# Token tile 2's transposed values copied out of PSUM by ScalarE, and the token differences moved behind the third ffn strip's weight split

## The chip, the cores and the metric

The kernel runs on one core of a Trainium2 chip. The metric is device time in microseconds (us) for one execution of the whole two-layer trunk. TensorE (PE in the profile, with its weight loads as PEld) does the matmuls, VectorE is DVE, ScalarE is ACT, GpSimd is POOL, and SyncE (SP) issues the DMAs. Each engine runs its own instruction list in order, and the lists are tied together by semaphores.

## What is computed

Two layers of a decoder trunk over 512 tokens of width 1024, in float32. The change lies between the first residual sum and the feed-forward part:

```
x = x + rms_norm(mix, norm_mix_post[i])
h = rms_norm(x, norm_ffn_pre[i])
gate, up = split_cols(h @ w_ffn_in[i], (D_FF, D_FF))     # D_FF = 2816: 22 strips of 128 columns
f = (jax.nn.silu(gate) * up) @ w_ffn_out[i]
x = x + rms_norm(f, norm_ffn_post[i])
```

## The kernel before

The tokens are handled in four tiles of 128 (m = 0 to 3). Every matmul operand is split into a rounded part and a remainder (`w_hi`, `w_lo` of the weights, `h_hi`, `h_lo` of the activations), and each product is three matmuls (lines 800 to 802). ScalarE writes the rounded part (line 1189 for weights, line 1225 for `h`), and VectorE subtracts it from the source to get the remainder (line 1603 for weights, line 1669 for `h`).

The order of the work is written out by hand: `plan_schedule` makes one list of events, and each engine walks through that same list and does its own share of each event. So an event's place in the list fixes what stands ahead of it on every engine that has a share in it.

For the ffn input, tile m goes through this chain. `post mix m` updates `x`. `pre ffn m` norms it: ScalarE takes a Square with its sum (line 1216), GpSimd turns the sum into a factor (lines 1481 and 1482), VectorE writes `xn` in two halves (line 1619). `T ffn m`: TensorE transposes `xn` into PSUM banks 2m and 2m+1 (line 993), ScalarE writes `h_hi`, VectorE writes `h_lo`.

The ffn strips 0, 1 and 2 (`f[0]`, `f[1]`, `f[2]`) are plain: a block `mm f[j] m` is 48 matmuls of 256 tokens, for token half m. Its first matmuls wait for the strip's `w_lo` (`lo_ready`, line 862). From strip 3 on, the kernel uses a scheme of seven products that needs, besides `h`, four combinations of `h` between the token halves, T_sum 1 to 4. The difference events make them on VectorE (`differences`, line 1673): `diff p 0` makes the first two from PSUM banks 4+2p and 5+2p (tile 2+p) and from `h_raw` (tile p), `diff p 1` makes the other two (lines 1680 and 1681). `h_raw` holds ScalarE's full-width copies of tiles 0 and 1 (event `hraw m`, line 1266); before each copy ScalarE waits until VectorE has read the same bank for `h_lo` (line 1265). Event `Tc` then splits T_sum into `T_hi` (line 1272) and `T_lo` (line 1767).

The block `mm f[2] 0` writes banks 4 and 5, where tile 2's transposed values lie, so it waits until `diff 0 0` has read them (line 955). SyncE loads the weights in pieces into five buffers, and reloads a buffer once VectorE has split the piece in it (line 775).

Of the kernel before, what the change touches and what calls it, by code (L numbers as in the profile page):

```python
# [16 lines left out]
F32 = mybir.dt.float32  # L17
# [7 lines left out]
P = 128  # L25
# [106 lines left out]
def plan_schedule(depth):  # L132


    ev = []
    strips = {kind: [s for s in STRIPS if s[0] == kind] for kind, _, _ in STRIPS}
    ins, o, f, fo, g = (strips[kind] for kind in ("in", "out", "ffn", "fo", "gate"))
    ple = ("ple", None, 0)
    layer = 0

    def add(*e, lay=None):
        ev.append((layer if lay is None else lay, e))

    def mm(strip, m, lay=None):
        add("mm", strip, m, lay=lay)

    def close(strip):

        add("conv", SIDX[strip] + SLOTS)

    def tail(pair, renew, after):

        lay = layer + (after == "mix")
        for m in range(TILES):
            mm(pair[0], m)
            if m >= 1:
                add(*renew, m - 1)
            if m >= 2 and after != "mix":  # L160
                add("T", after, m - 2, lay=lay)
                if m == TILES - 1 and after == "ffn":
                    add("hraw", 0)
                    close(pair[0])
            if m >= 1 and after == "ffn":
                add("pre", after, m - 1, lay=lay)
            if m == TILES - 1 and after != "ffn":
                close(pair[0])
            mm(pair[1], m)
            if m >= 1 and after == "mix" and lay < depth:  # L170
                add("T", after, m - 1, lay=lay)
                if m < TILES - 1:
                    add("pre", after, m - 1, lay=lay)

    for e in (("T", "mix", 0), ("conv", 0), ("mm", ins[0], 0), ("T", "mix", 1), ("pre", "mix", 0), ("T", "mix", 2),
              ("evac", ins[0], 0), ("pre", "mix", 1), ("mm", ins[0], 1), ("T", "mix", 3), ("conv", 1), ("pre", "mix", 2),
              ("evac", ins[0], 1), ("mm", ins[0], 2), ("pre", "mix", 3), ("mm", ins[0], 3), ("evac", ins[0], 2),
              ("conv", 2), ("mm", ins[1], 0), ("evac", ins[0], 3), ("mm", ins[1], 1)):
        add(*e)
    close(ins[0])  # L180
    for layer in range(depth):
        at = plan_mixers()
        u = 4
        for s in ins[1:]:
            for m in range(TILES):
                if u >= 6:
                    mm(s, m)
                for e in at.pop(u, ()):
                    add(*e)
                u += 1  # L190
            close(s)
        mm(o[0], 0)
        for u in (52, 53):
            if u == 53:
                mm(o[1], 0)
            for e in at.pop(u, ()):
                add(*e)
        add("gmlp_mix")
        mm(o[0], 1)
        mm(o[1], 1)  # L200
        add("gmlp_yT")
        mm(o[0], 2)
        mm(o[1], 2)
        assert not at, at
        mm(o[0], 3)
        close(o[0])
        mm(o[1], 3)
        close(o[1])
        tail(o[2:], ("post", "mix"), "ffn")
        add("post", "mix", 3)  # L210
        add("hraw", 1)
        add("hi", SIDX[f[2]])
        mm(f[0], 0)
        add("T", "ffn", 2)
        add("diff", 0, 0)
        add("pre", "ffn", 3)
        add("lo", SIDX[f[2]])
        add("diff", 0, 1)
        mm(f[1], 0)
        add("T", "ffn", 3)  # L220
        add("diff", 1, 0)
        add("diff", 1, 1)
        mm(f[2], 0)
        mm(f[0], 1)
        add("Tc")
        add("mid", 0)
        add("first")
        mm(f[1], 1)
        add("mid", 1)
        mm(f[2], 1)  # L230
        add("mid", 2)
        for j in FAST:
            add("step", j)
            if LAST - 5 <= j < LAST - 1:
                add("split", j - LAST + 5)
        add("last7")
        mm(fo[0], 3)
        add("last4")
        add("conv", SIDX[fo[1]])
        add("split", 4)  # L240
        add("split", 5)
        for m in (0, 1, 2):
            mm(fo[0], m)
        add("conv", SIDX[fo[2]])
        close(fo[0])
        add("split", 6)
        add("split", 7)
        for i in range(1, len(fo) - 2):
            for m in (2, 3, 0, 1):
                mm(fo[i], m)  # L250
            close(fo[i])
            for k in (2 * i + 6, 2 * i + 7):
                if k < FCH:
                    add("split", k)
        tail(fo[-2:], ("post", "ffn"), "gate")
        add("post", "ffn", 3)
        mm(ple, 0)
        add("T", "gate", 2)
        mm(ple, 1)
        add("T", "gate", 3)  # L260
        add("post", "ple", 0)
        mm(ple, 2)
        add("post", "ple", 1)
        close(fo[-1])
        mm(ple, 3)
        add("post", "ple", 2)
        add("post", "ple", 3)
        close(ple)
        for s in g[:2]:
            for m in range(TILES):  # L270
                mm(s, m)
            close(s)
        tail(g[2:], ("gated",), "mix")
        nxt = layer + 1
        if nxt < depth:
            add("gated", 3)
            mm(ins[0], 0, nxt)
            close(g[3])
            mm(ins[0], 1, nxt)
            add("T", "mix", 3, lay=nxt)  # L280
            add("pre", "mix", 2, lay=nxt)
            add("pre", "mix", 3, lay=nxt)
            mm(ins[0], 2, nxt)
            mm(ins[1], 0, nxt)
            mm(ins[1], 1, nxt)
            mm(ins[0], 3, nxt)
            add("conv", SIDX[ins[0]] + SLOTS, lay=nxt)
        else:
            add("gated", 3)
    return ev  # L290
# [44 lines left out]
def build_trunk(nc, depth, x_in, p_t, pre_mix, w_in, ln_w, ln_b, ws_t, bs_t, gn_w, sinks, w_out,  # L335
# [5 lines left out]
    def place(name, shape, dt, kb):  # L341
        return nc.alloc_sbuf_tensor_at(name, shape, dt, offset=BASE + int(kb * KB))
# [10 lines left out]
    T_sum = place("T_sum", [P, 4, 4, S // 2], F32, 64)  # L353
    ext_sum = place("ext_sum", [P, 3 * 512], F32, 130)
    h_raw = place("h_raw", [P, 2, 4, S // 2], F32, 116)
    ext_hi = place("ext_hi", [P, 3 * 512], F32R, 124)
    ext_lo = place("ext_lo", [P, 3 * 512], F32R, 130)
    w_sum = [place(f"w_sum{i}", [P, 2 * PIECE], F32, 172 + 8 * i) for i in range(SLOTS)]
# [372 lines left out]
    with nc.Block() as block:  # L731
# [66 lines left out]
        def _(pe):  # L798
# [133 lines left out]
            def block_of(layer, strip, m):  # L932
# [17 lines left out]
                    last = mm_rows(y_hi, y_lo, 2 * i, g, m, i == 3, i == 0)  # L950
                elif kind == "ffn":
                    if m == 0 and i < 2:
                        pe.wait_ge(h_raw_ready, 4 * layer + 2 * i + 2)
                    elif m == 0:
                        pe.wait_ge(t_raw, 8 * layer + 2)
                    last = mm_ffn(layer, g, strip, m)
                elif kind == "fo":
                    if i == 0 and m < 3:
                        pe.wait_ge((st_silu1, st_silu2, st_mid1)[m], nth(layer, LAST))
                    pe.wait_ge(mid_lo_ready, layer * FCH + 2 * i + 2)  # L960
                    last = mm_fo(g, i, m)
                elif kind == "ple":
                    pe.wait_ge(h_lo_ready, t_count(layer, "gate", m))
                    pe.wait_ge(p_lo_ready, layer + 1)
                    last = mm_rows(p_hi, p_lo, 0, g, m, True, True)
                else:
                    if i == 0:
                        pe.wait_ge(ple_ready, layer * TILES + m + 1)
                    if i == 3 and ends(layer, m):
                        last = mm_end(g)  # L970
                    else:
                        last = mm_rows(h_hi, h_lo, 2 * i, g, m, i == 0, i == 3)
# [185 lines left out]
        def _(act):  # L1158
# [90 lines left out]
            for layer, e in schedule:  # L1249
# [12 lines left out]
                elif kind == "hraw":  # L1262
                    m = e[1]
                    for half in range(2):
                        act.wait_ge(h_lo_ready, t_count(layer, "ffn", m, half))
                        act.activation(h_raw[:, half, :, m * P:(m + 1) * P],
                                       banks[2 * m + half][:, :].rearrange("p (k t) -> p k t", k=4),
                                       ACT.Copy).then_inc(h_raw_ready, 1)
                elif kind == "Tc":
                    for i in range(4):  # L1270
# [293 lines left out]
        def _(dve):  # L1564
# [108 lines left out]
            def differences(layer, p, part):  # L1673

                cols = slice(p * P, (p + 1) * P)
                top, low = (banks[4 + 2 * p + i][:, :].rearrange("p (k t) -> p k t", k=4) for i in range(2))
                t1, t2, t3, t4 = (T_sum[:, i, :, cols] for i in range(4))
                if part:
                    landed(combos["T2"])
                    done(dve.tensor_tensor(t3, t2, h_raw[:, 0, :, cols], ALU.subtract), t_raw)  # L1680
                    done(dve.tensor_tensor(t4, h_raw[:, 1, :, cols], t2, ALU.subtract), t_raw)
                    return
                dve.wait_ge(h_raw_ready, 4 * layer + 2 * p + 2)
                landed(done(dve.tensor_tensor(t1, top, h_raw[:, 0, :, cols], ALU.subtract), t_raw))
                combos["T2"] = done(dve.tensor_tensor(t2, low, t1, ALU.subtract), t_raw)

# [356 lines left out]
```

## Time and profile before

| | us |
|---|---|
| median of 3 runs | 1246.45 (1246.43 to 1246.53) |
| profiled execution, its own time | 1246.74 |
| its span in the profile | 1244.9 |
| TensorE busy in the span | 1236.6 |
| VectorE busy | 786.8 |
| ScalarE busy | 571.7 |
| GpSimd busy | 131.3 |

The profile is of one execution. The span is the time from its first to its last instruction; the profiled execution's own time has 1.84 us around it. A matmul's row shows a start and a modelled end that lies over the start of the next, so TensorE is best read by the starts of its matmuls. Times in rows are microseconds from the span's start. The stretch of interest lies at about 204 to 245 us in the first layer and at about 820 to 861 us in the second.

### The profile page before, as it was taken

The numbers are of one execution on the slowest core, as the hardware profiler recorded it, in microseconds if no ns is written. First come the engines' busy times: TensorE is split into PE (matmuls) and PEld (weight loads), VectorE is DVE, ScalarE is ACT, GpSimd is POOL, SyncE is SP. The second block draws the span as 40 slices with busy tenths as digits, with TensorE's granted clock in tenths as the row PEclk, the third lists the DMA queues.
The fourth block names the chain that finished last, engine by engine and source line by source line (L and its number), as shares of the span: only waits on it lengthen the run. The fifth ranks groups of instructions, "written<-read, shape, count | busy, mean of one in ns | idle before, by whom it ended". The sixth has DMA issues, their size and how long they took to land.

```text
span 1244.9 us, 20535 instructions
## 1 busy us (share of the span) xinstructions
PE 1236.6 (99%) x8045; PEld 1136.7 (91%) x8045; DVE 786.8 (63%) x1329; ACT 571.7 (46%) x1084; POOL 131.3 (11%) x225
## 2 busy tenths in 40 slices
PE   9999999999999999999999999999999999999998
PEld 7999888999999988888899989889999999888886
DVE  5575545888888843337466746368988887532463
ACT  6444334555555532235454444263655555322351
POOL 2003521100000000002120037120000000000020
PEclk9999999999999999999999999999999999999999
DMA  7322132233333353322232222231333332523211
GB/s 248 104 65 89 69 102 68 69 102 102 102 108 112 104 170 102 131 72 89 77 96 62 89 65 85 85 97 57 102 108 112 105 103 102 170 85 134 68 51 67
DMA packets 124206, 122.30 MB, mean 98 GB/s; under 512 B 5200, under 2 KB 109008, under 8 KB 124112
## 3 DMA queue, kind: packets, MB, share of 16 engines
q1 hardware_dynamic: 124112, 121.01, 31.2%
q8 instruction: 64, 1.05, 0.3%
q14 instruction: 30, 0.25, 0.1%
HBM read 118.90 MB, written 2.10 MB: 97 GB/s over the span
## 4 chain that ended last, share of the span: by engine, by line
PE 99%; DVE 0%; DMA 0%; SPq 0%; issue 0%; ACT 0%; ACTq 0%
PE bank L800 30%; PE bank L802 30%; PE bank L801 30%; PE bank L993 2%; PE bank L1050 1%; PE bank L1073 1%; PE bank L1119 1%; PE bank L1071 1%; PE bank L1103 1%; PE bank L1058 0%; PE bank L1095 0%; PE bank L1115 0%; DMA raw<-in_w_in 0%; PE bank L1124 0%; PE bank L1145 0%; PE bank L1032 0%
## 5 line engine op out<-in xcount | busy, mean ns | idle before, releaser
L800 PE MATMUL bank<-w_hi,h_hi 128*128 128x384 f32 (+2 forms) x672 | 244.0, 363 | 1.8 <-DVE w_lo L1605 1.8
L801 PE MATMUL bank<-w_lo,h_hi 128*128 128x384 f32 (+2 forms) x672 | 237.5, 353 | 0.0
L802 PE MATMUL bank<-w_hi,h_lo 128*128 128x384 f32 (+2 forms) x576 | 200.4, 348 | 0.0
L1603 DVE TENSOR_TENSOR w_lo<-raw,w_hi 128x1024 fp32r<-128x1024 f32 x86 | 102.4, 1230 | 150.0 <-ACT w_hi L1189 149.8
L1189 ACT ACTIVATE w_hi<-raw 128x1024 fp32r<-128x1024 f32 x86 | 86.7, 1055 | 174.5 <-PE bank L802 174.4
L800 PE MATMUL bank<-h_hi,w_hi 128*128 128x256 f32 x568 | 161.0, 284 | 0.5 <-issue 0.5
L802 PE MATMUL bank<-h_hi,w_lo 128*128 128x256 f32 x568 | 160.7, 283 | 0.0
L801 PE MATMUL bank<-h_lo,w_hi 128*128 128x256 f32 x568 | 160.7, 283 | 0.0
L800 PEld LDWEIGHTS bank<-w_hi,h_hi 128*128 128x128 f32 x672 | 126.4, 188 | 15.5 <-issue 1.7
L802 PE MATMUL bank<-w_hi,mid_lo 128*128 128x512 f32 x352 | 137.0, 389 | 0.0
L801 PEld LDWEIGHTS bank<-w_lo,h_hi 128*128 128x128 f32 x672 | 126.6, 188 | 10.7
L800 PE MATMUL bank<-T_hi,w_hi 128*128 128x256 f32 x448 | 126.8, 283 | 0.0
L801 PE MATMUL bank<-T_lo,w_hi 128*128 128x256 f32 x448 | 126.8, 283 | 0.0
L802 PE MATMUL bank<-T_hi,w_lo 128*128 128x256 f32 x448 | 126.8, 283 | 0.0
L802 PEld LDWEIGHTS bank<-w_hi,h_lo 128*128 128x128 f32 x576 | 108.3, 188 | 7.6
L800 PEld LDWEIGHTS bank<-h_hi,w_hi 128*128 128x128 f32 x568 | 109.0, 192 | 1.0 <-issue 0.9
L801 PEld LDWEIGHTS bank<-h_lo,w_hi 128*128 128x128 f32 x568 | 109.0, 192 | 0.1
L802 PEld LDWEIGHTS bank<-h_hi,w_lo 128*128 128x128 f32 x568 | 109.0, 192 | 0.0
L1247 ACT ACTIVATE w_hi<-w_sum 128x512 fp32r<-128x512 f32 x112 | 70.5, 629 | 52.5 <-DVE w_sum L1703 51.2
L1502 POOL TENSOR_SCALAR tiny<-tiny 128x1 f32<-128x1 f32 x24 | 13.1, 544 | 763.8 <-ACT junk_f L1340 676.0
L1605 DVE SCALAR_TENSOR_TENSOR w_lo<-raw,mix_col,w_hi 128x384 fp32r<-128x384 f32 (+2 forms) x112 | 63.6, 630 | 38.1 <-ACT w_hi L1189 38.1
L800 PEld LDWEIGHTS bank<-T_hi,w_hi 128*128 128x128 f32 x448 | 86.0, 192 | 0.0
(235 smaller groups left out, 2665.6 us busy)
## 6 DMA issues: line engine op xcount, KB each, us to landing
raw<-in_w_ffn_in SPq DMA_DIRECT2D x88, 512.0 KB, 3.8
raw<-in_w_ffn_out SPq DMA_DIRECT2D x44, 512.0 KB, 3.3
raw<-in_w_in SPq DMA_DIRECT2D x40, 384.0 KB, 3.7
raw<-in_w_out SPq DMA_DIRECT2D x16, 512.0 KB, 4.0
raw<-in_w_gate SPq DMA_DIRECT2D x16, 512.0 KB, 4.1
raw<-in_w_in SPq DMA_DIRECT2D x10, 512.0 KB, 4.1
raw<-in_w_ple SPq DMA_DIRECT2D x4, 512.0 KB, 5.1
x<-in_x_in SPq DMA_DIRECT2D x3, 512.0 KB, 6.9
```

The lines of the kernel that those rows point to most:

```text
L800: pe.matmul(out_ap, a_hi, b_hi, start=start, stop=False, skip_group_check=True)
L801: pe.matmul(out_ap, a_hi, b_lo, start=False, stop=False, skip_group_check=True)
L802: return pe.matmul(out_ap, a_lo, b_hi, start=False, stop=stop, skip_group_check=True)
L993: last = pe.transpose(banks[2 * m + half][:, k * P:(k + 1) * P], src[:, kk * P:(kk + 1) * P], T_("ident"))
L1050: last = pe.matmul(swa_bank(c, g)[:, j * P:(j + 1) * P], cT[rows(g), j, ts(c)], cT[rows(g), 3, ts(k0)], start=True, stop=True, skip_group_ ...
L1071: pe.matmul(o, ptu[c % 2][:, hh, :], cv[:, c - 1, g, :], start=True, stop=False, skip_group_check=True)
L1073: last = pe.matmul(o, ptl[c % 2][:, hh, :], dv[:, c % 2, g, :] if c else cv[:, 0, g, :], start=(c == 0), stop=True, skip_group_check=True)
L1189: last = act.activation(w_hi[slot_of(g)][:, j * n + cols.start:j * n + cols.stop], raw[q % RAWS][:, cols], ACT.Copy, scale=1.0 if col is N ...
L1247: act.activation(hi, whole, ACT.Copy).then_inc(st_hi, 1)
L1502: step(pool.tensor_scalar(t_post, ss_post[n % 2][:, 0:1], ss_post[n % 2][:, 1:2], EPS, ALU.add, ALU.add))
L1603: last = dve.tensor_tensor(lo, raw[q % RAWS][:, cols], hi, ALU.subtract)
L1605: last = dve.scalar_tensor_tensor(out=lo[:, cols], in0=raw[q % RAWS][:, cols], scalar=col, in1=hi[:, cols], op0=ALU.mult, op1=ALU.subtract)
```

## The change

ScalarE gets two more copies in each layer (`hraw 2`): it copies tile 2's two banks into a new buffer `h_raw2`, each after VectorE has read that bank for `h_lo`. This event stands between `T ffn 2` and `pre ffn 3`. `diff 0 0` reads the new buffer instead of the banks, and moves from ahead of `pre ffn 3` to behind the weight split of strip 2. The block `mm f[2] 0` waits for ScalarE's copies instead of for the two differences. The semaphore counts follow from six copies in a layer instead of four.

```diff
         add("T", "ffn", 2)
-        add("diff", 0, 0)
+        add("hraw", 2)
         add("pre", "ffn", 3)
         add("lo", SIDX[f[2]])
+        add("diff", 0, 0)
         add("diff", 0, 1)
...
+    h_raw2 = place("h_raw2", [P, 2, 4, P], F32, 60)
...
                     if m == 0 and i < 2:
-                        pe.wait_ge(h_raw_ready, 4 * layer + 2 * i + 2)
+                        pe.wait_ge(h_raw_ready, 6 * layer + 2 * i + 2)
                     elif m == 0:
-                        pe.wait_ge(t_raw, 8 * layer + 2)
+                        pe.wait_ge(h_raw_ready, 6 * layer + 6)
...
                         act.wait_ge(h_lo_ready, t_count(layer, "ffn", m, half))
-                        act.activation(h_raw[:, half, :, m * P:(m + 1) * P],
-                                       banks[2 * m + half][:, :].rearrange("p (k t) -> p k t", k=4),
+                        dst = h_raw2[:, half, :, :] if m == 2 else h_raw[:, half, :, m * P:(m + 1) * P]
+                        act.activation(dst, banks[2 * m + half][:, :].rearrange("p (k t) -> p k t", k=4),
                                        ACT.Copy).then_inc(h_raw_ready, 1)
...
-                top, low = (banks[4 + 2 * p + i][:, :].rearrange("p (k t) -> p k t", k=4) for i in range(2))
+                top, low = (banks[6 + i][:, :].rearrange("p (k t) -> p k t", k=4) if p else h_raw2[:, i, :, :]
+                            for i in range(2))
...
-                dve.wait_ge(h_raw_ready, 4 * layer + 2 * p + 2)
+                dve.wait_ge(h_raw_ready, 6 * layer + (4 if p else 6))
```

ScalarE's list between the weight split of strip 2 and the start of strip 3, first layer. The `h_hi` rows are the rounding of tile 2 and of tile 3, the `junk` row is the Square of tile 3. Before:

```order
L1266 ACTIVATE h_raw<-bank 128x4x128 x2
L1189 ACTIVATE w_hi_76<-raw_73 128x1024
L1189 ACTIVATE w_hi_76<-raw_74 128x1024
L1225 ACTIVATE h_hi<-bank 128x4x128 x2
L1216 ACTIVATE junk,tiny<-x 128x1024
L1225 ACTIVATE h_hi<-bank 128x4x128 x2
L1272 ACTIVATE T_hi<-T_sum 128x1024 x4
```

Now:

```order
L1269 ACTIVATE h_raw<-bank 128x4x128 x2
L1191 ACTIVATE w_hi_77<-raw_74 128x1024
L1191 ACTIVATE w_hi_77<-raw_75 128x1024
L1227 ACTIVATE h_hi<-bank 128x4x128 x2
L1269 ACTIVATE h_raw_60<-bank 128x512 x2
L1218 ACTIVATE junk,tiny<-x 128x1024
L1227 ACTIVATE h_hi<-bank 128x4x128 x2
L1274 ACTIVATE T_hi<-T_sum 128x1024 x4
```

Two copies (`h_raw_60` is the new buffer) have come in ahead of tile 3's Square.

VectorE's list over the same place. The first `h_lo` row is tile 2, the second is tile 3; `xn` is tile 3. Before:

```order
L1856 TENSOR_TENSOR x<-x,upd 128x1024
L1669 TENSOR_TENSOR h_lo<-bank,h_hi 128x4x128 x2
L1684 TENSOR_TENSOR T_sum<-bank,h_raw 128x4x128
L1685 TENSOR_TENSOR T_sum<-bank,T_sum 128x4x128
L1619 SCALAR_TENSOR_TENSOR xn_126<-x,tiny,pre_w 128x512 x2
L1603 TENSOR_TENSOR w_lo_79<-raw_73,w_hi_76 128x1024
L1603 TENSOR_TENSOR w_lo_79<-raw_74,w_hi_76 128x1024
L1680 TENSOR_TENSOR T_sum<-T_sum,h_raw 128x4x128
L1681 TENSOR_TENSOR T_sum<-h_raw,T_sum 128x4x128
L1669 TENSOR_TENSOR h_lo<-bank,h_hi 128x4x128 x2
```

Now:

```order
L1859 TENSOR_TENSOR x<-x,upd 128x1024
L1671 TENSOR_TENSOR h_lo<-bank,h_hi 128x4x128 x2
L1621 SCALAR_TENSOR_TENSOR xn_127<-x,tiny,pre_w 128x512 x2
L1605 TENSOR_TENSOR w_lo_80<-raw_74,w_hi_77 128x1024
L1605 TENSOR_TENSOR w_lo_80<-raw_75,w_hi_77 128x1024
L1687 TENSOR_TENSOR T_sum<-h_raw_60,h_raw 128x4x128
L1688 TENSOR_TENSOR T_sum<-h_raw_60,T_sum 128x4x128
L1683 TENSOR_TENSOR T_sum<-T_sum,h_raw 128x4x128
L1684 TENSOR_TENSOR T_sum<-h_raw,T_sum 128x4x128
L1671 TENSOR_TENSOR h_lo<-bank,h_hi 128x4x128 x2
```

The two differences of tile 2 have moved from ahead of `xn` to behind the two halves of strip 2's `w_lo`. The second layer has the same lists; TensorE's, GpSimd's and SyncE's lists are as they were.

## Rows read from the trace of the kernel before

**Rows 1.** The page: busy time by engine, and TensorE's granted clock in 40 slices.

```profile
PE 1236.6 (99%) x8045; PEld 1136.7 (91%) x8045; DVE 786.8 (63%) x1329; ACT 571.7 (46%) x1084; POOL 131.3 (11%) x225
...
PEclk9999999999999999999999999999999999999999
```

**Rows 2.** Timeline, PE, tile 3's transposes: start, length, engine, line, operation [idle before].

```profile
230.12 1.03 PE L993 MATMUL bank<-tab,xn 128*128 128x128 f32 x8
231.40 0.36 PE L800 MATMUL bank<-h_hi,w_hi 128*128 128x256 f32 x1 [0.25 <-issue]
231.59 0.28 PE L801 MATMUL bank<-h_lo,w_hi 128*128 128x256 f32 x1
```

**Rows 3.** Timeline, PE, tile 2's transposes and the matmul two behind them.

```profile
223.49 1.03 PE L993 MATMUL bank<-tab,xn 128*128 128x128 f32 x8
...
224.48 0.28 PE L801 MATMUL bank<-h_lo,w_hi 128*128 128x256 f32 x1
```

**Rows 4.** Timeline, DVE, first layer, from tile 3's `x` to the first `mid`.

```profile
225.10 1.23 DVE L1856 TENSOR_TENSOR x<-x,upd 128x1024 f32<-128x1024 f32 x1
226.24 1.28 DVE L1669 TENSOR_TENSOR h_lo<-bank,h_hi 128x512 fp32r<-128x512 f32 x2
227.44 0.68 DVE L1684 TENSOR_TENSOR T_sum<-bank,h_raw 128x512 f32<-128x512 f32 x1
...
228.76 1.40 DVE L1619 SCALAR_TENSOR_TENSOR xn<-x,tiny,pre_w 128x512 f32<-128x512 f32 x2
230.09 2.35 DVE L1603 TENSOR_TENSOR w_lo<-raw,w_hi 128x1024 fp32r<-128x1024 f32 x2
232.36 0.68 DVE L1680 TENSOR_TENSOR T_sum<-T_sum,h_raw 128x512 f32<-128x512 f32 x1
...
233.56 1.28 DVE L1669 TENSOR_TENSOR h_lo<-bank,h_hi 128x512 fp32r<-128x512 f32 x2
...
237.52 4.63 DVE L1767 TENSOR_TENSOR T_lo<-T_sum,T_hi 128x1024 fp32r<-128x1024 f32 x4
243.81 0.69 DVE L1879 TENSOR_TENSOR mid<-silu_g,bank 128x512 f32<-128x512 f32 x1 [1.66 <-ACT silu_g L1371]
```

**Rows 5.** Timeline, ACT, tile 1's copies, the next split, and tile 3's Square.

```profile
221.19 1.08 ACT L1266 ACTIVATE h_raw<-bank 128x512 f32<-128x512 f32 x2
222.14 2.02 ACT L1189 ACTIVATE w_hi<-raw 128x1024 fp32r<-128x1024 f32 x2
...
226.36 1.06 ACT L1216 ACTIVATE junk<-x 128x1024 bf16<-128x1024 f32 x1 [1.15 <-DVE x L1856]
```

**Rows 6.** Timeline, POOL: the last step of tile 3's factor.

```profile
227.90 0.57 POOL L1482 TENSOR_TENSOR tiny<-tiny 128x1 f32<-128x1 f32 x1
```

**Rows 7.** Timeline, ACT, DVE and PE: tile 0's chain, from Square to matmul.

```profile
204.07 1.06 ACT L1216 ACTIVATE junk<-x 128x1024 bf16<-128x1024 f32 x1 [3.88 <-DVE x L1856]
...
206.22 1.42 DVE L1619 SCALAR_TENSOR_TENSOR xn<-x,tiny,pre_w 128x512 f32<-128x512 f32 x2 [2.18 <-POOL tiny L1482]
...
207.03 1.33 PE L993 MATMUL bank<-tab,xn 128*128 128x128 f32 x8
...
208.43 0.39 PE L801 MATMUL bank<-w_lo,y_hi 128*128 128x512 f32 x1
```

**Rows 8.** Timeline, all engines: tile 2's chain, beside a weight split on DVE.

```profile
218.60 2.35 DVE L1603 TENSOR_TENSOR w_lo<-raw,w_hi 128x1024 fp32r<-128x1024 f32 x2
...
218.71 1.06 ACT L1216 ACTIVATE junk<-x 128x1024 bf16<-128x1024 f32 x1
...
219.95 1.08 POOL L1481 TENSOR_SCALAR tiny<-tiny 128x1 f32<-128x1 f32 x1 [5.10 <-ACT junk L1216]
...
221.72 1.42 DVE L1619 SCALAR_TENSOR_TENSOR xn<-x,tiny,pre_w 128x512 f32<-128x512 f32 x2 [0.77 <-POOL tiny L1482]
```

**Rows 9.** Timeline, DVE and PE, the same place in the second layer.

```profile
844.73 1.40 DVE L1619 SCALAR_TENSOR_TENSOR xn<-x,tiny,pre_w 128x512 f32<-128x512 f32 x2
...
847.56 0.28 PE L801 MATMUL bank<-h_lo,w_hi 128*128 128x256 f32 x1
```

## The prediction

> **What bounds the kernel now.** I read the busy times first. TensorE is busy for 1236.6 of the span's 1244.9 us and its granted clock is full in every slice, while VectorE has 786.8 us of work and ScalarE 571.7 [rows 1]. So the time is TensorE's list plus the holes in it. An edit on another engine changes the time only if it closes or opens a hole there. I then read the starts of TensorE's matmuls, since a modelled end hides small holes. In the stretch that the change touches there is one: behind the eight transposes of tile 3. From their first start to the second matmul behind them it takes 231.59 - 230.12 = 1.47 us [rows 2]; at tile 2, where nothing is late, the same stretch takes 224.48 - 223.49 = 0.99 us [rows 3]. The hole is 0.48 us. VectorE's list shows who closes it: the first half of strip 2's `w_lo`, which starts at 230.09, two of them in 2.35 us, so the first ends near 231.3 [rows 4], just before the matmul at 231.40 [rows 2]. The second layer has the same pattern [rows 9]. The most that an earlier `w_lo` can bring is thus 2 x 0.48 = 0.96 us.
>
> The chain into that point is: `x` of tile 3, ScalarE's Square, GpSimd's factor, VectorE's `xn`, then `w_lo` on VectorE and the transposes on TensorE. The Square starts at 226.36, right behind VectorE's `x` [rows 5]. The factor is ready at 227.90 + 0.57 = 228.47 [rows 6]. `xn` starts at 228.76, since VectorE is busy with `diff 0 0` from 227.44 until then [rows 4].
>
> **The differences go behind the split.** They take 228.76 - 227.44 = 1.32 us of VectorE [rows 4]. Alone, this move would let `xn` start as soon as the factor is there: 228.47 instead of 228.76, so 0.29 us earlier, not 1.32, because the factor is next. `w_lo` would follow 0.29 us earlier and the hole would shrink by about that. Over two layers this is 0.6 us gained. The differences cost the same from the copy as from the banks, as far as rows tell: one with both inputs in SBUF takes 0.68 us, as one with an input in PSUM does [rows 4].
>
> **ScalarE's two copies.** They stand ahead of tile 3's Square, and ScalarE works in order. Each waits for VectorE's `h_lo` on the same bank. The pair of `h_lo` starts at 226.24 and ends at 227.52 [rows 4]; its first ends about 0.6 earlier, near 226.9. The first copy thus starts near 226.95. The second can't start before 227.52 plus the hand-over, about 0.03 as from `x` to the Square (`x` ends at 225.10 + 1.23 = 226.33 [rows 4], the Square starts at 226.36 [rows 5]), so at 227.55. How long does it hold the next instruction? A pair of such copies holds it 222.14 - 221.19 = 0.95 us [rows 5], so one holds it 0.48, or 0.6 at most (the pair's 1.08 less the first's 0.48). I take 0.50, since the next starts a little before the copy's end in those rows. The Square starts at 228.05, which is 1.69 us later than before. The bounds are 1.65 and 1.80.
>
> **From the Square to the matmul.** For tile 0 the chain from Square to `xn` takes 206.22 - 204.07 = 2.15 us, with VectorE waiting for the factor [rows 7]. VectorE would again be waiting here: behind `h_lo`, at 227.44, the next in its list is now `xn`. So `xn` starts at 228.05 + 2.15 = 230.20, against 228.76: 1.44 us later. Everything in VectorE's list up to `w_lo` hangs on it directly: 230.09 - 228.76 = 1.33 us from `xn` to `w_lo` [rows 4], so `w_lo` starts at 231.53. From there to TensorE's second matmul it was 231.59 - 230.09 = 1.50 us, so that stands at 233.03 instead of 231.59.
>
> Is something on TensorE later still? Its transposes wait for the first half of `xn`, and start 207.03 - 206.22 = 0.81 us behind its start [rows 7]. That is 231.01, 0.9 us after TensorE has arrived (230.12). From the transposes to the second matmul, with their second half also waiting, it takes 208.43 - 207.03 = 1.40 us, so 232.41. That is before 233.03. The wait for the transposes lies inside the wait for `w_lo`, and the loss is 1.44 us for the layer. The new wait for ScalarE's copies (over at 228.15) costs nothing.
>
> **Behind it.** On VectorE, `w_lo` holds the next for 232.36 - 230.09 = 2.27 us. Then come both difference events and tile 3's `h_lo`. The latter starts at 231.53 + 2.27 + 1.32 + 1.20 = 236.32 (1.20 is 233.56 - 232.36) and ends at 237.60 [rows 4]. Its reader is the next block, `mm f[0] 1`, one block of 48 matmuls behind 233.0. Such a block takes about the 230.12 - 224.48 = 5.64 us of 47 matmuls [rows 2, 3], so it starts at 238.6 or later, and TensorE does not wait. `T_lo` starts at 231.53 + 2.27 + 1.32 + (237.52 - 232.36) = 240.28, 2.76 late, while TensorE and all that hangs on it are 1.44 late. The surplus of 1.32 us meets an idle stretch of 1.66 us ahead of the first `mid` [rows 4]. It just fits, with 0.3 to spare; past that, the strip 3 preparation would slide, which has TensorE's blocks `f[1] 1` and `f[2] 1` (over 11 us) as cover. The loads behind `w_lo` are issued 1.44 us later, in step with TensorE; the first reader stands in the step of strip 3, behind these same blocks. SyncE and GpSimd get nothing new.
>
> **The second layer.** From `xn` to the second matmul behind the transposes it takes 847.56 - 844.73 = 2.83 us there [rows 9], and 231.59 - 228.76 = 2.83 us in the first layer [rows 2, 4]. The lists are the same, so I take the same loss again, 1.44 us.
>
> **The sum.** 2 x 1.44 = 2.9 us slower. The bounds with copies of 0.48 to 0.60 and chain steps read to 0.05 us are 2.7 to 3.2. The profiled execution would go from 1246.74 to 1249.6, its span from 1244.9 to 1247.8. The median of the runs is 0.29 us under the profiled execution, so I forecast 1246.45 + 2.9 = 1249.35 us. A measurement of this kernel tells about 0.2% from no change, which is 2.5 us here: the forecast lies 0.4 us over that line.
>
> **Rivals.**
> 1. The gain arrives: the copies don't hold the Square, and only the differences' move is felt. The hole shrinks by 0.29 to 0.48 us per layer: 1245.5 to 1245.9. The place is ScalarE ahead of tile 3's Square: from a Square at 228.76 - 2.15 = 226.61 or earlier on, `xn` is no later than before, and the kernel does not get slower. It would need the Square to start ahead of copies that stand before it in the list, so the list speaks against it. 5%.
> 2. The copies cost less than I count, because the factor or `xn` makes up some of the delay. To fall below the 2.5 us line, 0.2 us per layer must come back. The chain of 2.15 us is the shorter of the two in the rows, and the copies' start is tied to `h_lo`. Time: 1247.9 to 1248.9. 11%.
> 3. The chain from Square to `xn` is longer. Tile 2's takes 221.72 - 218.71 = 3.01 us, since GpSimd's first step lasts 1.08 us, until just after VectorE's weight split (218.60 to 220.95) ends [rows 8]. If GpSimd is held up so at tile 3 too, each layer loses 0.86 more: 1251.1. But VectorE would be idle there. 6%. The Trainium skill (SBUF — State Buffer, "Who interferes with whom") states that a VectorE instruction with two SBUF inputs and a GpSimd instruction that reads SBUF exclude one another, the second waiting for the first. By that rule the trace of tile 2 is explained, and the differences, which now have two SBUF inputs, would be a danger to tile 3's factor had they stayed ahead of `xn`; where they stand now it gives 2.15.
> 4. TensorE's granted clock falls, as it now stands still for up to 0.9 and 0.6 us in a row. It was full across all the trace, waits at the start among it [rows 1]. Some us more, 2%.
> 5. The forecast, 1249.35: 74%. The last 2% is for something unseen that makes it faster.
>
> **Range and chances.** The forecast's own case spans 1249.1 to 1249.7. To hold 8 in 10 the range reaches up to the longer chain, 1251.2, and down over half of rival 2, 1248.4. Slower by over 0.2%: 74 + 6 + 2 = 82, less 2 for the part of the forecast's case near the line, 80%. Within 0.2%: 5 + 11 + 2 = 18%. Faster: 2%.
>
> **What would show it.** In the profile after, the two copies start near 226.95 and 227.55, the Square near 228.05, `xn` near 230.2 after some 2.7 us of VectorE idling for GpSimd, the transposes of tile 3 near 231.0, and the second matmul behind them near 233.0. The first `mid` stands near 245.3 with almost no idle time before it. If the Square stands earlier, the copies' step is wrong; if `xn` stands later than 2.15 behind it, the chain's; if TensorE's time from there to the end grows by more than the 2.9, the cover behind it was not enough. A stalled `mid` that reaches TensorE would make it wrong upward, copies that overlap the Square downward.

## The result and the profile after

The changed kernel takes 1249.45 us (median of 10 runs, 1249.25 to 1250.02) against 1246.37 us for the kernel before (1246.09 to 1246.53). The ratio is 1.0025, with a 95% interval of 1.0017 to 1.0034. Measured again beside two of its variants it took 1249.48 us against 1246.40, ratio 1.0023 (1.0014 to 1.0033). So it is 3.1 us slower; the forecast was 1249.35, 2.9 us slower. Both intervals lie above 1, but both take in 1.002: that the kernel is slower is clear of the noise, that it is slower by more than 0.2% is not.

The profiled execution has a span of 1247.6 us against 1244.9. Line numbers after are two or three higher than before: the Square is line 1218, `xn` 1621, a weight split 1605, the new copies 1269, the transposes 995.

ScalarE's timeline of the changed kernel in the first layer; the columns are start, length, engine, line, operation and the idle time before it with what ended it. The first row is tile 2's `h_hi`.

```profile
224.02 1.09 ACT L1227 ACTIVATE h_hi<-bank 128x512 fp32r<-128x512 f32 x2
226.84 1.19 ACT L1269 ACTIVATE h_raw<-bank 128x512 f32<-128x512 f32 x2 [1.73 <-DVE h_lo L1671]
227.93 1.05 ACT L1218 ACTIVATE junk<-x 128x1024 bf16<-128x1024 f32 x1
```

The copies stand where [rows 5] had the Square waiting for `x`, and they wait for `h_lo`. A narrower window of the same view parts the pair:

```profile
226.84 0.60 ACT L1269 ACTIVATE h_raw<-bank 128x512 f32<-128x512 f32 x1 [1.73 <-DVE h_lo L1671]
...
227.43 0.60 ACT L1269 ACTIVATE h_raw<-bank 128x512 f32<-128x512 f32 x1
```

The Square starts at 227.93 instead of 226.36, 1.57 us later. GpSimd and VectorE follow:

```profile
229.15 0.22 POOL L1483 TENSOR_SCALAR tiny<-tiny 128x1 f32<-128x1 f32 x1 [5.71 <-ACT junk L1218]
229.46 0.57 POOL L1484 TENSOR_TENSOR tiny<-tiny 128x1 f32<-128x1 f32 x1
```

```profile
224.97 1.23 DVE L1859 TENSOR_TENSOR x<-x,upd 128x1024 f32<-128x1024 f32 x1
226.12 1.28 DVE L1671 TENSOR_TENSOR h_lo<-bank,h_hi 128x512 fp32r<-128x512 f32 x2
230.06 1.42 DVE L1621 SCALAR_TENSOR_TENSOR xn<-x,tiny,pre_w 128x512 f32<-128x512 f32 x2 [2.66 <-POOL tiny L1484]
231.39 2.35 DVE L1605 TENSOR_TENSOR w_lo<-raw,w_hi 128x1024 fp32r<-128x1024 f32 x2
233.66 0.68 DVE L1687 TENSOR_TENSOR T_sum<-h_raw,h_raw 128x512 f32<-128x512 f32 x1
...
235.11 0.69 DVE L1683 TENSOR_TENSOR T_sum<-T_sum,h_raw 128x512 f32<-128x512 f32 x1
...
240.28 4.63 DVE L1770 TENSOR_TENSOR T_lo<-T_sum,T_hi 128x1024 fp32r<-128x1024 f32 x4
245.12 0.69 DVE L1882 TENSOR_TENSOR mid<-silu_g,bank 128x512 f32<-128x512 f32 x1 [0.20 <-ACT silu_g L1373]
```

Here `mid` is the product of `silu(gate)` and `up` for a strip. Set against [rows 4], VectorE, which was busy from `h_lo` to `xn`, now idles for 2.66 us until GpSimd has the factor, and `xn` starts 1.30 us later on the trace's clock. This trace is 0.13 us ahead there: its `x` starts at 224.97, against 225.10 in [rows 4]. So `xn` is 1.43 us later against its own `x`. TensorE pays for it in two places:

```profile
229.89 0.28 PE L804 MATMUL bank<-h_hi,w_lo 128*128 128x256 f32 x1
230.87 1.32 PE L995 MATMUL bank<-tab,xn 128*128 128x128 f32 x8 [0.70 <-DVE xn L1621]
232.71 0.36 PE L802 MATMUL bank<-h_hi,w_hi 128*128 128x256 f32 x1 [0.52 <-issue]
232.90 0.28 PE L803 MATMUL bank<-h_lo,w_hi 128*128 128x256 f32 x1
```

The last matmul ahead of the transposes starts at 229.89 and the transposes at 230.87. In the kernel before, the transposes followed such a matmul 0.12 us later, at 230.12 [rows 2] behind this one:

```profile
230.00 0.29 PE L802 MATMUL bank<-h_hi,w_lo 128*128 128x256 f32 x1
```

So 0.86 us is a wait for `xn`. From the transposes to the second matmul it takes 2.03 us, against 1.47 in [rows 2] and 0.99 where nothing waits [rows 3]. The two places together are 0.86 + 0.56 = 1.42 us. The second layer repeats it:

```profile
844.24 1.20 ACT L1269 ACTIVATE h_raw<-bank 128x512 f32<-128x512 f32 x2 [1.73 <-DVE h_lo L1671]
845.33 1.05 ACT L1218 ACTIVATE junk<-x 128x1024 bf16<-128x1024 f32 x1
...
850.30 0.28 PE L803 MATMUL bank<-h_lo,w_hi 128*128 128x256 f32 x1
```

That matmul stood at 847.56 [rows 9]; it is 2.74 us later, which is the whole difference of the spans (2.7). Nothing is lost behind it, and nothing given back.

### The profile page after: what moved, and what is told of

Read it like the earlier page. It is cut to its first block, busy times and chain, and to the rows that moved or that the text cites. A ratio compares the mean times of both kernels' runs of the same rounds, so it can differ in the third digit from the quotient of the medians.

```text
span 1247.6 us, 20539 instructions
## 1 busy us (share of the span) xinstructions
PE 1237.1 (99%) x8045; PEld 1136.5 (91%) x8045; DVE 787.1 (63%) x1329; ACT 573.9 (46%) x1088; POOL 131.1 (11%) x225
## 4 chain that ended last, share of the span: by engine, by line
PE 78%; DVE 2%; ACT 1%; issue 1%; POOL 1%; POOLq 0%; ACTq 0%
PE bank L802 25%; PE bank L804 25%; PE bank L803 25%; PE bank L995 1%; DVE upd L1847 1%; ACT junk L1218 1%; DVE x L1859 1%; PE bank L1052 0%; PE bank L1075 0%; PE bank L1121 0%; PE bank L1073 0%; DVE h_lo L1671 0%; PE bank L1105 0%; POOL tiny L1504 0%; ACT junk L1340 0%
```

## The experiments

My theory was that the two copies, ahead of tile 3's Square, delay the Square, the factor, `xn` and `w_lo` one after the other, while the move of the differences is free or a small gain. The main rival was that the moved differences, and the backlog that they make on VectorE behind the weight split, cost the time. All edits are shown against the changed kernel, if not said otherwise. The `add` lines are in `plan_schedule`; the other lines are in the part where the engine concerned walks through the list (ScalarE for `hold` and `hraw`, VectorE for `conv` and the added subtractions). Ratios are against the kernel before, measured in the same rounds: its median was 1246.45 us beside the Square first, the copies without the move, the wait alone and the added work, and 1246.40 beside one copy ahead, the half split and the repeated changed kernel. The start-up of the traces differs by up to 0.7 us, so each position is best read against `x` of tile 3 in its own trace.

### The Square first

```diff
         add("T", "ffn", 2)
-        add("hraw", 2)
         add("pre", "ffn", 3)
+        add("hraw", 2)
         add("lo", SIDX[f[2]])
         add("diff", 0, 0)
```

> The changed kernel with ScalarE's two new copies put behind tile 3's Square instead of ahead of it; the differences stay behind the weight split. My theory (the copies hold the Square, and through it the factor, xn and w_lo): the Square is back near 226.4, xn starts near 228.48, when GpSimd's factor is there, 0.28 us before its place in the kernel before, and the second matmul behind tile 3's transposes near 231.3. Time 0.56 us under the kernel before: 1245.8 us. Rival (the moved differences and the VectorE backlog behind the split cost the time): 1249.4 us, as in the changed kernel.

Measured: 1245.92 us, ratio 0.9994 (0.9986 to 1.0003). All of the loss is gone though the same copies and the same move of the differences are there, which rules out the rival. In this trace `x` of tile 3 starts at 224.78, 0.32 us ahead of [rows 4]. ScalarE's, VectorE's and TensorE's timelines of this kernel:

```profile
226.04 1.06 ACT L1218 ACTIVATE junk<-x 128x1024 bf16<-128x1024 f32 x1 [1.12 <-DVE x L1859]
227.01 0.19 ACT L1218 ACTIVATION_READ_ACCUMULATOR junk<-x 128x1 f32 x1
227.10 1.07 ACT L1269 ACTIVATE h_raw<-bank 128x512 f32<-128x512 f32 x2
```

```profile
228.19 1.41 DVE L1621 SCALAR_TENSOR_TENSOR xn<-x,tiny,pre_w 128x512 f32<-128x512 f32 x2 [0.98 <-POOL tiny L1484]
229.52 2.35 DVE L1605 TENSOR_TENSOR w_lo<-raw,w_hi 128x1024 fp32r<-128x1024 f32 x2
```

```profile
229.82 1.04 PE L995 MATMUL bank<-tab,xn 128*128 128x128 f32 x8
230.84 0.36 PE L802 MATMUL bank<-h_hi,w_hi 128*128 128x256 f32 x1
231.03 0.28 PE L803 MATMUL bank<-h_lo,w_hi 128*128 128x256 f32 x1
```

The copies now run while VectorE waits for GpSimd. From the transposes to the second matmul it is 1.21 us instead of 1.47, so 0.26 us of the 0.48 us hole per layer is closed. This is the gain of the differences' move where the copies hold up nobody, forecast at 0.29. The median is 0.53 us under the kernel before, the fastest of all versions here; but the interval takes in 1, so the times alone don't prove it faster. The trace shows where it would come from.

### The copies without the move

```diff
         add("T", "ffn", 2)
         add("hraw", 2)
+        add("diff", 0, 0)
         add("pre", "ffn", 3)
         add("lo", SIDX[f[2]])
-        add("diff", 0, 0)
```

> The changed kernel with the two differences of tile 2 back ahead of xn; they read ScalarE's copies, which stand ahead of the Square. My theory: the Square is at 228.0 as in the changed kernel, the differences run between 228.1 and 229.5 while the factor is made, so xn starts at 230.2: 1249.4 us. By the Trainium skill (SBUF - State Buffer, Who interferes with whom) GpSimd's first step waits for the differences, which now have two SBUF inputs: it would last about 0.4 instead of 0.22 us, xn at 230.4, time up to 1249.9 us. Rival (the move of the differences costs the time): 1246.4 us.

Measured: 1249.83 us, ratio 1.0027 (1.0017 to 1.0037). The loss is there without the move. It is 0.4 us above the changed kernel, near what the expectation gave for a GpSimd step held up by the differences. The two intervals overlap, so the times alone don't show these 0.4 us; the traces do, with 0.18 us in the first layer: from its own `x` (224.94) to `xn` it is 5.27 us here, and 230.06 - 224.97 = 5.09 in the changed kernel. VectorE's and GpSimd's timelines:

```profile
228.02 0.69 DVE L1687 TENSOR_TENSOR T_sum<-h_raw,h_raw 128x512 f32<-128x512 f32 x1 [0.66 <-ACT h_raw L1269]
228.75 0.69 DVE L1688 TENSOR_TENSOR T_sum<-h_raw,T_sum 128x512 f32<-128x512 f32 x1
230.21 1.42 DVE L1621 SCALAR_TENSOR_TENSOR xn<-x,tiny,pre_w 128x512 f32<-128x512 f32 x2 [0.77 <-POOL tiny L1484]
```

```profile
229.12 0.41 POOL L1483 TENSOR_SCALAR tiny<-tiny 128x1 f32<-128x1 f32 x1 [5.71 <-ACT junk L1218]
229.61 0.57 POOL L1484 TENSOR_TENSOR tiny<-tiny 128x1 f32<-128x1 f32 x1
```

GpSimd's first step lasts 0.41 us instead of 0.22, to 229.53; the second difference ends at 229.44.

### The wait without the copies

This one is against the kernel before: ScalarE waits for VectorE's `h_lo` of tile 2 and does nothing else.

```diff
         add("diff", 0, 0)
+        add("hold")
         add("pre", "ffn", 3)
...
+                elif kind == "hold":
+                    act.wait_ge(h_lo_ready, t_count(layer, "ffn", 2))
                 elif kind == "hraw":
```

> The kernel before, with one wait more and nothing else: ScalarE waits for VectorE's h_lo of tile 2 before tile 3's Square. It tells the wait of the copies from their length. My theory: the Square starts at 227.55 instead of 226.36, xn 2.15 behind it at 229.70 instead of 228.76, so 0.94 us per layer: 1248.3 us. If the length of the copies were what costs (0.5 us of holding each), the wait alone would change nothing: 1246.4 us.

Measured: 1248.35 us, ratio 1.0013 (1.0005 to 1.0022), against 1248.3 expected. So 1.9 us of the 3.1 is the order in which `h_lo` and the Square now stand, and by this it would be paid however short the copies were. The rest is mostly the second copy's holding the Square, which comes on top of the wait: 0.50 us in each layer (227.93 - 227.43 in the changed kernel). ScalarE's Square in this kernel, where `x` starts at 225.41, 0.31 us later than in [rows 4]:

```profile
227.87 1.06 ACT L1217 ACTIVATE junk<-x 128x1024 bf16<-128x1024 f32 x1 [2.32 <-DVE h_lo L1672]
```

### One copy ahead

```diff
-        add("hraw", 2)
+        add("hraw", 2, 0)
         add("pre", "ffn", 3)
+        add("hraw", 2, 1)
...
-                    for half in range(2):
+                    for half in (e[2:] or (0, 1)):
```

> The changed kernel with only the first of the two new copies ahead of tile 3's Square, the second behind it. My theory: the first copy starts at 226.9, when h_lo's first half is done, and holds the Square for 0.5, so the Square starts at 227.4 and xn at 229.55, 0.8 us late instead of 1.44: 1248.0 us. Rival (the differences' move costs): 1249.4 us.

Measured: 1248.06 us, ratio 1.0013 (1.0004 to 1.0022). The loss grows with the copies ahead: none, one and two give -0.5, +1.7 and +3.1 us. One copy costs a little less than the wait alone did, because it waits only for the first half of `h_lo`: the Square starts 2.35 us behind its own `x` (225.03) here, and 2.46 us with the wait alone. ScalarE:

```profile
226.89 0.60 ACT L1270 ACTIVATE h_raw<-bank 128x512 f32<-128x512 f32 x1 [1.73 <-DVE h_lo L1672]
227.38 1.05 ACT L1219 ACTIVATE junk<-x 128x1024 bf16<-128x1024 f32 x1
228.33 0.19 ACT L1219 ACTIVATION_READ_ACCUMULATOR junk<-x 128x1 f32 x1
228.43 0.59 ACT L1270 ACTIVATE h_raw<-bank 128x512 f32<-128x512 f32 x1
```

A copy of 0.60 us holds the next instruction for 0.49.

### Half of the weight split ahead of `xn`

Against the kernel with the Square first, to see if the rest of the hole can be closed:

```diff
+        add("lo", SIDX[f[2]], 0)
         add("pre", "ffn", 3)
         add("hraw", 2)
-        add("lo", SIDX[f[2]])
+        add("lo", SIDX[f[2]], 1)
...
-                    conv(layer * NS + e[1])
+                    conv(layer * NS + e[1], (e[2],))
```

> As the kernel with the Square first, and with the first half of strip 2's weight split put ahead of xn on VectorE, where it waits for GpSimd's factor. If GpSimd runs freely beside it: xn starts near 228.6, TensorE finds transposes and w_lo in time, no hole is left, 0.96 us under the kernel before: 1245.4 us. If the split holds GpSimd up as it did at tile 2 in the kernel before (a first step of 1.08 us, ending with the split; the Trainium skill, SBUF - State Buffer, Who interferes with whom, says so for two SBUF inputs): the first step ends near 228.7, xn starts near 229.4, second matmul behind tile 3's transposes at 231.6, as before: 1246.4 us.

Measured: 1246.25 us, ratio 0.9999 (0.9991 to 1.0008), so the second outcome. VectorE's and GpSimd's timelines, on a trace whose `x` starts at 225.35, 0.25 us later than in [rows 4]:

```profile
227.69 1.21 DVE L1606 TENSOR_TENSOR w_lo<-raw,w_hi 128x1024 fp32r<-128x1024 f32 x1
229.67 1.41 DVE L1622 SCALAR_TENSOR_TENSOR xn<-x,tiny,pre_w 128x512 f32<-128x512 f32 x2 [0.77 <-POOL tiny L1485]
```

```profile
227.84 1.14 POOL L1484 TENSOR_SCALAR tiny<-tiny 128x1 f32<-128x1 f32 x1 [4.03 <-ACT junk L1219]
229.07 0.57 POOL L1485 TENSOR_TENSOR tiny<-tiny 128x1 f32<-128x1 f32 x1
```

GpSimd's first step, otherwise 0.22 us, ends at 228.98, just behind the split's end at 228.90. VectorE's free time could not be used for this: the work that filled it held up the engine that it waits for.

### More work behind the split

```diff
                         done(dve.tensor_tensor(T_lo[:, i, :, :], T_sum[:, i, :, :],
                                                T_hi[:, i, :, :].bitcast(F32), ALU.subtract), t_lo)
+                    for _ in range(2):
+                        step(dve.tensor_tensor(h_raw[:, 0, :, :], h_raw[:, 0, :, :], h_raw[:, 1, :, :], ALU.subtract))
```

> The changed kernel with two needless differences of 1024 elements on VectorE behind T_lo in each layer, some 2.6 us, where only 0.2 us of idle time is left ahead of the first mid. My theory (the backlog behind the weight split has TensorE's blocks f[1] 1 and f[2] 1 as cover): no change against the changed kernel, 1249.45 us. Rival (the backlog already reaches TensorE): up to 2.4 us per layer more, 1254 us.

Measured: 1249.83 us, ratio 1.0026 (1.0017 to 1.0035). That is 0.4 us above the changed kernel, not the 4.8 that two layers of 2.4 us would add, and the two intervals overlap. The first `mid` in VectorE's timeline stands at 247.08, 2.2 us later than in the changed kernel if each is read against its own `x` (224.71 here, 224.97 there):

```profile
240.02 4.63 DVE L1770 TENSOR_TENSOR T_lo<-T_sum,T_hi 128x1024 fp32r<-128x1024 f32 x4
244.57 2.47 DVE L1773 TENSOR_TENSOR h_raw<-h_raw 128x1024 f32<-128x1024 f32 x2
247.08 0.69 DVE L1884 TENSOR_TENSOR mid<-silu_g,bank 128x512 f32<-128x512 f32 x1
...
256.38 0.69 DVE L1884 TENSOR_TENSOR mid<-silu_g,bank 128x512 f32<-128x512 f32 x1 [1.49 <-ACT silu_g L1373]
```

By the third `mid` VectorE is waiting again, and this `mid` is 31.67 us behind its own `x` as in the changed kernel (256.64 there), so the backlog is gone before it reaches TensorE. The trace has a loss in another place. In the second layer, ahead of the Square, VectorE's `upd` of tile 3 (the residual update that `x` waits for) starts after an idle gap of 0.86 us instead of the 0.51 us that this gap takes in the changed kernel. Here first the changed kernel's rows, with the GpSimd step that makes the factor for `upd`, then this one's:

```profile
840.01 0.84 POOL L1506 TENSOR_TENSOR tiny<-tiny 128x1 f32<-128x1 f32 x1
840.93 1.41 DVE L1847 SCALAR_TENSOR_TENSOR upd<-bank,tiny,post_w 128x512 f32<-128x512 f32 x2 [0.51 <-issue]
```

```profile
839.72 0.84 POOL L1506 TENSOR_TENSOR tiny<-tiny 128x1 f32<-128x1 f32 x1
841.00 1.41 DVE L1849 SCALAR_TENSOR_TENSOR upd<-bank,tiny,post_w 128x512 f32<-128x512 f32 x2 [0.86 <-issue]
```

The gap of 0.51 us is a wait for GpSimd, though the row says `issue`: `upd` starts 0.08 us behind the factor's end at 840.85. In this kernel it starts 0.44 us behind the factor's end at 840.56, and no row shows what the other 0.36 us wait for. They go through `x`, the copies and the Square to TensorE, whose wait at tile 3's transposes is 1.06 instead of 0.70 us in that layer. Why they are there stays open; the extra instructions shift all that stands behind them in VectorE's list, but no run parts that from chance. Nor is it shown that they are the 0.4 us of the medians: the profiled execution took 1249.43 us, the shortest of this kernel's eleven.

### The changed kernel beside its variants

> The changed kernel itself, on the same chip as its variants. 1249.4 us.

Measured: 1249.48 us (1248.89 to 1249.67), ratio 1.0023 (1.0014 to 1.0033).

## Why the prediction was right

**What bounds it.** That only TensorE's holes count held: the matmul behind the hole is 2.74 us later in the second layer, and the span 2.7 us longer.

**The copies.** They were to start at 226.95 and 227.55, and the Square at 228.05. They start at 226.84, 227.43 and 227.93, on a trace that is 0.13 us ahead, so each is met within 0.02 us. The wait alone costs 1.9 us, as worked out beforehand from [rows 4] and [rows 5]; the full pair costs 3.1 us, where 2.9 were worked out.

**The chain.** 2.15 us from Square to `xn` was taken; it is 230.06 - 227.93 = 2.13. The longer one of 3.01 us did not come, for the reason given: VectorE was idle while GpSimd worked. Two experiments made VectorE busy there with two inputs from SBUF, and the chain grew, to 2.32 and 3.06 us.

**The later of two waits on TensorE.** The transposes were to start at 231.01 and the second matmul at 233.03. They are at 230.87 and 232.90, again with the 0.13 us. The loss in the first layer is 232.90 - 231.59 + 0.13 = 1.44 us.

**The differences' move.** Expected 0.29 us of gain per layer if it stood alone; the kernel with the Square first shows 0.26.

**The cover behind it.** The first `mid` was to have 0.3 us to spare; it has 0.20. The term of 1.32 us for the moved differences was too small here: with `T_sum` 3 behind them they held VectorE for 235.11 - 233.66 = 1.45 us. That cost nothing, and 2.5 us of more work there did not reach TensorE either.

**The size.** 2.9 was forecast and 3.1 measured. How much of that the traces hold can be read without the start-up, from ScalarE's first Square to its last. First the kernel before, then the changed one:

```profile
12.88 1.06 ACT L1216 ACTIVATE junk<-x 128x1024 bf16<-128x1024 f32 x1
...
1198.09 0.59 ACT L1340 ACTIVATE junk<-bank 128x512 bf16<-128x512 f32 x1
```

```profile
12.79 1.06 ACT L1218 ACTIVATE junk<-x 128x1024 bf16<-128x1024 f32 x1
...
1200.83 0.59 ACT L1342 ACTIVATE junk<-bank 128x512 bf16<-128x512 f32 x1
```

That is 1185.21 and 1188.04 us, so 2.83 us more, which is the forecast. The same reading for all kernels, beside the medians:

| Kernel | median less the kernel before's, us | first to last Square, less the kernel before's, us |
|---|---|---|
| changed | 3.08 | 2.83 |
| changed, repeated | 3.08 | 2.80 |
| copies without the move | 3.38 | 3.20 |
| more work behind the split | 3.38 | 3.14 |
| wait without the copies | 1.90 | 1.87 |
| one copy ahead | 1.66 | 1.63 |
| half of the split ahead | -0.15 | -0.21 |
| Square first | -0.53 | -0.51 |

The two columns agree within 0.06 us, except in the kernels with both copies ahead of the Square, where the medians are 0.2 to 0.3 us longer than the traces. That is the difference between 3.1 and 2.9, and where it lies stays open: it can be in the start-up, which the second column leaves out and which differs from trace to trace (the first Square starts between 12.54 and 13.21), or in waits that the profiled executions happened not to have. In the kernel before, the chain through GpSimd had 0.29 us of slack against VectorE's differences, and now it has none, so a lateness on that chain would now reach TensorE; that this makes the 0.2 us is argued, not shown.

## What to carry to other kernels

Before putting an instruction into a free stretch of an engine, read what ends that stretch and what stands behind it. ScalarE had over 1 us free here, but the next in its list was the head of a chain over four engines into TensorE, and the copies waited for an event that came after that head could have run. The same copies one place further down cost nothing. Where a stall is to be removed, name the next late event first: moving 1.32 us of work off the path could bring only 0.29, as another engine's result was due then.

## What the runs showed of the hardware

GpSimd's step of one column, 0.22 us long when VectorE is idle, lasts until the end of VectorE's subtraction of two SBUF tensors when it starts beside one: 1.08 us in [rows 8], and 1.14 us and 0.41 us in two experiments, ending 0.08 to 0.09 us behind it. Beside a difference with one input in PSUM it kept its 0.22 us, as in the kernel before, where `diff 0 0` ran on VectorE from 227.44 to 228.12 [rows 4]:

```profile
227.59 0.22 POOL L1481 TENSOR_SCALAR tiny<-tiny 128x1 f32<-128x1 f32 x1 [4.03 <-ACT junk L1216]
```

The Trainium skill (SBUF — State Buffer, "Who interferes with whom") states this rule for VectorE instructions with two SBUF inputs against GpSimd instructions that read SBUF; the traces agree. It makes a copy out of PSUM double-edged: the difference takes 0.68 to 0.69 us from SBUF as from PSUM, but from SBUF it held GpSimd up, for 0.19 us.

TensorE's granted clock stayed at its full level, 2.4 GHz (1.00 in the stretches from 229 to 232 and from 232 to 235 us), with waits of 0.86 and about 1 us in each layer; it was 1.00 from 842 to 852 us too.
